# Page numbers of a decoder kernel: 64 loads into registers per layer, against sixteen packed words loaded once

## What is computed

```python
# _mix, for the sample group; past['k'] is (80 pages, 2 layers, 128, 8, 64)
pk = past['k'][past['page_table'], l].reshape(B, -1, SB_HEADS, SB_HEAD_DIM)
pv = past['v'][past['page_table'], l].reshape(B, -1, SB_HEADS, SB_HEAD_DIM)
P = pk.shape[1]
o_b = _sb_attend(q, concatenate([pk, k]), concatenate([pv, v]),
                 P + arange(T), arange(P + T), sbb)
# page_table: 64 of a permutation of 80, as int32
```

## Time and profile before

| | |
|---|---|
| median of 3 runs | 2043.45 us (2041.63 to 2048.05) |
| the profiled execution: its time | 2043.22 us |
| its span in the profile | 2041.4 us |
| busy share of the span | PE 91%, PEld 77%, DVE 47%, ACT 35%, POOL 4% |
| DMA | 391.48 MB, mean 192 GB/s |
| mean granted TensorE clock | 0.947 of full |

### The profile page before, as it was taken

One profiled execution on the slowest core, in us unless ns is written; L12 is line 12 of the kernel. 1 busy time (PEld: TensorE's weight loads), 2 busy tenths in 40 slices (PEclk: granted clock), 3 DMA queues, 4 the chain that ended last, 5 costly groups with the idle time before them and its releaser, 6 DMA issues. The chain is left out here.

```text
span 2041.4 us, 33570 instructions
## 1 busy us (share of the span) xinstructions
PE 1851.3 (91%) x12436; PEld 1567.1 (77%) x12436; DVE 965.1 (47%) x1749; ACT 720.3 (35%) x1317; POOL 81.7 (4%) x111
## 2 busy tenths in 40 slices
PE   6999989999987897999969999899999878979997
PEld 4988966776765686998959888667767656869997
DVE  4555425335355534555355553253353644346554
ACT  3554323323321103554345443233233211046552
POOL 0000010000000001000010000100000000010001
PEclk7999989999998998999979999999999888989999
DMA  7777642462348922456547776342641588325561
GB/s 320 279 281 293 252 170 84 167 232 109 134 154 211 272 104 101 166 200 254 226 165 271 299 292 227 146 161 81 237 183 59 165 256 224 110 99 174 213 229 69
DMA packets 87842, 391.48 MB, mean 192 GB/s; under 512 B 14402, under 2 KB 19778, under 8 KB 57410
## 3 DMA queue, kind: packets, MB, share of 16 engines
q1 hardware_dynamic: 72738, 368.24, 50.8%
q10 hardware_dynamic: 15008, 21.95, 2.9%
HBM read 377.32 MB, written 12.83 MB: 191 GB/s over the span
## 5 line engine op out<-in xcount | busy, mean ns | idle before, releaser
L982 DVE TENSOR_TENSOR ring_parts<-ring,pages_parts 128x1024 fp32r<-128x1024 f32 (+1 forms) x272 | 314.3, 1191 | 199.2 <-ACT pages_parts L1539 199.1
L451 PE MATMUL ps<-xn,ring 128*128 128x264 f32 x1664 | 400.0, 401 | 6.1 <-ACT xn L1546 6.1
L490 PE MATMUL ps<-arena_parts,pages_parts 128*128 128x264 f32 x1408 | 361.4, 292 | 23.5 <-DVE xn_parts L1050 21.1
L451 PEld LDWEIGHTS ps<-xn,ring 128*128 128x128 f32 x1664 | 326.9, 199 | 70.0 <-issue 10.4
L491 PE MATMUL ps<-xn_parts,pages_parts 128*128 128x264 f32 x1408 | 357.0, 288 | 0.0
L1539 ACT ACTIVATE pages_parts<-ring 128x1024 fp32r<-128x1024 f32 (+1 forms) x272 | 267.8, 1025 | 179.8 <-DMA ring<-in_w_ffn_in 71.8
L490 PEld LDWEIGHTS ps<-arena_parts,pages_parts 128*128 128x128 f32 x1408 | 271.8, 193 | 44.2 <-issue 43.6
L491 PEld LDWEIGHTS ps<-xn_parts,pages_parts 128*128 128x128 f32 x1408 | 271.2, 193 | 0.0
L495 PE MATMUL ps<-arena_parts,ring_parts 128*128 128x264 f32 x1408 | 196.5, 283 | 0.0
L490 PE MATMUL ps<-big_parts,pages_parts 128*128 128x264 f32 x704 | 177.6, 288 | 6.6 <-DVE gates_parts L996 6.6
L495 PEld LDWEIGHTS ps<-arena_parts,ring_parts 128*128 128x128 f32 x1408 | 181.9, 188 | 0.0
(11 more groups left out here) (312 smaller groups left out, 2039.6 us busy)
## 6 DMA issues: line engine op xcount, KB each, us to landing
ring<-in_w_ffn_in SPq DMA_DIRECT2D x88, 1024.0 KB, 4.9
ring<-in_w_ada SPq DMA_DIRECT2D x32, 1536.0 KB, 6.5
ring<-in_w_a SPq DMA_DIRECT2D x32, 1536.0 KB, 11.1
ring<-in_w_ffn_down SPq DMA_DIRECT2D x32, 1408.0 KB, 6.5
pages<-in_k_pages SPq DMA_DIRECT2D x128, 256.0 KB, 5.0
pages<-in_v_pages SPq DMA_DIRECT2D x128, 256.0 KB, 6.2
ring<-in_w_ada SPq DMA_DIRECT2D x24, 1024.0 KB, 7.2
ring<-in_w_proj SPq DMA_DIRECT2D x8, 1536.0 KB, 9.4
```

The source lines that it names most:

```text
L451: last = mm(ps[:, b, 0:T], tile_of(r, first + k), rhs(k), start=(k == 0), stop=(k == depth - 1))
L490: mm(ps[:, b, 0:T], tile, hi[:, k, :], start=start, stop=False)
L982: v.tensor_tensor(ring_lo[:, r, at * P:(at + n) * P], w, whi[:, place, 0:n * P].bitcast(F32), ALU.subtract)\
```

## The change

The DMA of the table now takes only the low byte of each number, 64 elements of one byte, so that four numbers lie in one 32-bit word of `ptab`. `read_tables` loads the sixteen words into sixteen registers once, in the first layer, after the loop over the first 16 FFN tiles. `page_number` takes a number out of its word with a shift and a mask, two register operations just ahead of the page's DMA. It is called between the wait and the issue. The hardware loop over the four heads is written out, since a register can't be chosen by a loop's index.

```diff
-        ptab = sb("ptab", [1, NB * PAGES], I32)
+        ptab = sb("ptab", [1, NB * PAGES // 4], I32)
+        ptab_bytes = ptab[:].bitcast(mybir.dt.uint8)
...
-                    sp.dma_start(ptab[:], ins.page_table).then_inc(S.t_in, 16)
+                    sp.dma_start(ptab_bytes.unsqueeze(2), ins.page_table.bitcast(mybir.dt.uint8)
+                                 .rearrange("p (n b) -> p n b", b=4)[:, :, 0:1],
+                                 allow_slow_non_contiguous=True).then_inc(S.t_in, 16)
...
+                def read_tables():
+
+                    sp.wait_ge(S.t_in, 48)
+                    packed.extend(sp.value_load(ptab[0:1, w:w + 1], min_val=0, max_val=(1 << 31) - 1)
+                                  for w in range(NB * PAGES // 4))
+
+                def page_number(n):
+
+                    number = sp.alloc_register()
+                    sp.reg_alu(number, packed[n // 4], 8 * (n % 4), ALU.logical_shift_right)
+                    sp.reg_alu(number, number, 127, ALU.bitwise_and)
+                    return sp.snap(number, donate=True, min_val=0, max_val=PHYS - 1)
...
+                if first_layer:
+                    read_tables()
                 for k in range(16, FC):
                     load(ins.w_ffn_in[layer, 0, k], 2)
...
-                if first_layer:
-                    sp.wait_ge(S.t_in, 48)
-                with sp.Fori(0, HEADS) as i, slots.loop(i, HEADS, [3] * 4), page_loads.loop(i, HEADS, 2):
-                    for k in range(3):
-                        load(ins.w_a[layer, i * 4 + k], 3)
-                    sp.wait_ge(S.yss_ready, 1)
-                    load_pages(ins.k_pages, i * 2)
-                    load(ins.w_a[layer, i * 4 + 3], 3)
-                    load_pages(ins.k_pages, i * 2 + 1)
...
+                for i in range(HEADS):
+                    for k in range(3):
+                        load(ins.w_a[layer, i * 4 + k], 3)
+                    sp.wait_ge(S.yss_ready, 1)
+                    load_key_pages(i * 2)
+                    load(ins.w_a[layer, i * 4 + 3], 3)
+                    load_key_pages(i * 2 + 1)
```

More of the change, by code:

```diff
@@ L291, in clear_all @@
             nc.all_engine_barrier()
+        packed = []
         def one_layer(block, layer):
@@ L307, in _ @@
             def _(sp):
-                slots, page_loads = Slots(), Count()
+                slots = Slots()
                 def start_loads():
@@ L331, in load @@
                     sp.dma_start(ring[:, r, 0:tiles * P], src).then_inc(slot_full[r], 16)
-                def load_pages(pool_of_pages, b):
-                    before = page_loads()
-                    numbers = [sp.value_load(ptab[0:1, bds(b * PAGES + j, 1)], min_val=0, max_val=PHYS - 1)
-                               for j in range(PAGES)]
-                    for j, page in enumerate(numbers):
-                        if j % 2 == 0:
-                            sp.wait_ge(page_free[j // 2], before + 1)
-                        sp.dma_start(pages[:, j, :], pool_of_pages[layer, page]).then_inc(page_full[j // 2], 16)
+                def read_tables():
[7 more added lines that the diff above has]
+                    return sp.snap(number, donate=True, min_val=0, max_val=PHYS - 1)
                 if first_layer:
@@ L361, in _, with load_key_pages, load_value_pages @@
                     load(ins.w_sq[layer, s], 2)
-                if first_layer:
-                    sp.wait_ge(S.t_in, 48)
-                with sp.Fori(0, HEADS) as i, slots.loop(i, HEADS, [3] * 4), page_loads.loop(i, HEADS, 2):
+                def load_key_pages(b):
+                    for j in range(PAGES):
+                        if j % 2 == 0:
+                            sp.wait_ge(page_free[j // 2], b + 1)
+                        sp.dma_start(pages[:, j, :], ins.k_pages[layer, page_number(b * PAGES + j)])\
+                            .then_inc(page_full[j // 2], 16)
+                def load_value_pages(b):
+                    for u in range(2):
+                        if b == 0:
+                            for j in range(4):
+                                sp.wait_ge(page_free[j], 2 * HEADS + 1)
+                        else:
+                            sp.wait_ge(value_free[u], b)
+                        for j in range(4):
+                            sp.dma_start(pages[:, 2 * j + u, :], ins.v_pages[layer, page_number(b * PAGES + 2 * j + u)])\
+                                .then_inc(value_full[u], 16)
+                for i in range(HEADS):
                     for k in range(3):
@@ L367, in _ @@
                     sp.wait_ge(S.yss_ready, 1)
-                    load_pages(ins.k_pages, i * 2)
+                    load_key_pages(i * 2)
                     load(ins.w_a[layer, i * 4 + 3], 3)
-                    load_pages(ins.k_pages, i * 2 + 1)
-                def load_value_pages(b):
-                    numbers = [sp.value_load(ptab[0:1, b * PAGES + j:b * PAGES + j + 1], min_val=0, max_val=PHYS - 1)
-                               for j in range(PAGES)]
-                    for u in range(2):
-                        if b == 0:
-                            for j in range(4):
-                                sp.wait_ge(page_free[j], page_loads.n + 1)
-                        else:
-                            sp.wait_ge(value_free[u], b)
-                        for j in range(4):
-                            sp.dma_start(pages[:, 2 * j + u, :], ins.v_pages[layer, numbers[2 * j + u]])\
-                                .then_inc(value_full[u], 16)
+                    load_key_pages(i * 2 + 1)
                 load(ins.w_b[layer, 0], 2)
```

## The result

| | before | after |
|---|---|---|
| median of 8 runs each | 2044.45 us (2041.63 to 2049.65) | 2058.6 us (2049.9 to 2064.55) |
| ratio, with its 95% interval | | 1.0068 [1.0049, 1.0086] |
| the profiled execution: its time | 2043.22 us | 2058.02 us |
| its span | 2041.4 us | 2056.2 us |
| mean granted TensorE clock | 0.947 | 0.949 |

A forecast was written before the change was run, and what follows sets the result against it. TensorE, busy 91% of 2041.4 us, was taken as the bound. 2043.2 - 0 (loads) + 1.4 (page operations) + 2.0 (FFN stall) + 0 (table DMA) = 2046.6, so 2046.8 against the median, 0.16% slower; range 2039 to 2052.5.

The forecast's parts named there:

- Sixteen loads take 9.0 us: First FFN: sixteen loads at 0.56 us each come ahead of tile 16's issue, ending at 140.9 with the branch.
- A tile needs 7.17 us from issue to its first piece: First FFN: time from a tile's issue to the end of VectorE's first piece, taken from tile 17; tile 16 ready at 148.1.
- TensorE began tile 16 at 146.09, so it needs it then: First FFN: tile 16, ready at 148.1, would stall TensorE once, +2.0 us, with ends of 0 and 4.0.
- The clock: nothing added, 0.9 or more at the upper end: TensorE's granted clock after the FFN stall: no loss added for a 2.0 us gap, 0.9 us or more at the upper end.
- For key pages this is hidden (no DMA wait at all): First mixer half: two register operations per page, 0.16 us, cost nothing; value pages pay 0.16 for each of nine waits, +1.4 us.
- upper end of 5.8: Second mixer half: the most the register operations on value pages could cost, 9 x 0.64 = 5.8 us.
- Gain from the 256 loads: 0: Mixer: removing the 256 register loads gains 0, with a bound of 3.5 us per layer, 7.
- Rival 3: Second mixer half: value sample 2's lateness was passed on, 3.5 us in each layer, so 2039.8; 9%.
- rival 2: Second mixer half: register loads slow the DMAs; some 23 us of waits would go, time near 2023; 5%.
- Rival 1, the byte elements: Start: the table's 64 one-byte elements block the DMA queue at 17 us, loads behind come 4.6 us later, 2051.4; 18%.

The follow-up runs named there:

- before_loads16: The kernel before with sixteen unused page-number loads added behind the loop over the first 16 FFN tiles of layer 1; 2048.54 us, ratio 1.0032.
- rows_first: The changed kernel with VectorE's copy to rbuf put ahead of its split of tile 16, the sixteen loads left in place; 2059.82 us, ratio 1.0053 to the kernel before.
- before_unrolled: The kernel before with its mixer loop over four heads written out, all 256 register loads kept; 2048.45 us, ratio 0.9995.
- mask_keys: The kernel before, loop written out, all loads kept, two register operations that change nothing ahead of each key page's DMA only; ratio 1.0010.
- late_ahead: The changed kernel with its sixteen loads moved into the mixer's first head and page numbers taken apart ahead of the waits; 2050.54 us, ratio 1.0015 to the kernel before.
- unrolled_mask: The kernel before, loop written out, all loads kept, two register operations that change nothing ahead of every page's DMA; 2048.2 us, ratio 1.0024.
- mask_values: The kernel before, loop written out, all loads kept, two register operations that change nothing ahead of each value page's DMA only; ratio 1.0002.
- fixed_pages: before_unrolled with constants for page numbers, so no register loads or operations for them and other pages read; 2042.76 us, ratio 0.9991 to the kernel before.
- late_table: late_ahead with the table's byte DMA issued behind the first FFN's loads, start waits for masks and sel alone; ratio 1.0024 to the kernel before.
- read_late: The changed kernel with its sixteen loads moved into the mixer's first head, behind the second load of w_a; 2046.27 us, ratio 1.0021 to the kernel before.

## Why the prediction was wrong, step by step

**"Sixteen loads take 9.0 us": right in kind, 0.5 short.** The timeline has 132.19 + 0.33 = 132.52 to 142.27, less the branch: 9.5 us or 0.59 each. The instructions are as long as in the earlier trace rows (a TENSOR_LOAD of 267 ns in the median, from 262 to 470). The lateness of 0.7 us that SyncE brings from the start comes on top, so tile 16 went out at 142.3 instead of 140.9. The figure of the Trainium skill, page "DMA: Bandwidth & Descriptors", section "Latency and other measured facts", some 600 ns for one `tensor_load`, would by the forecast's estimate have given 14 us. The measurement stands against it as a figure for the instruction, as the rows before did; a whole number, with its register operation, its check and the gaps, took 0.59 us.

**"A tile needs 7.17 us from issue to its first piece": right.** 142.27 to VectorE's first piece, which starts at 148.24 and takes half of 2.36, is 7.15 us.

**"TensorE began tile 16 at 146.09, so it needs it then": the step that failed.** The sum asked when TensorE wants the tile. It didn't ask what else stands behind the tile's split on VectorE. The copy to `rbuf` does (line 959 before), behind both pieces and not the first alone, and TensorE wants it before the tile. With the forecast's own numbers the right chain gives 140.9 + 7.17 + 1.18 (second piece) = 149.25, and 149.8 with the copy (0.55), against 145.84: a stall of 4.0, not 2.0. before_loads16 measured 4.21, and rows_first, with the order changed, 2.44.

**"The clock: nothing added, 0.9 or more at the upper end": mis-sized.** The stall was treated as nearer the short gap of the earlier trace rows, 1.20 us, and came out near the long one, 5.23. 1.7 us (1.3 in before_loads16) were lost behind it. A stall of the forecast's size might not have spared the clock either: in rows_first the gap was 2.44 us, and the granted clock was 0.50 from 149 to 152. Stall and clock are 6.3 us in the changed kernel's trace, and 6.5 by before_loads16's ratio.

**"For key pages this is hidden (no DMA wait at all)": the second step that failed.** That no wait is seen says that the room is not negative; it doesn't say how large it is. It was 0.16 to 0.91 us, less than what was added. The 0.16 us per page were right: the eight issues take 3.94 us in before_unrolled and 5.00 to 5.42 in mask_keys, 0.15 to 0.21 more per step. But the forecast counted only the first page's 0.16 for each wait, where TensorE waits for the last of eight, which comes 1.2 later. mask_keys shows the waits (3.3 us) and late_ahead takes them away (0). That they are most of the time lost is argued from these sums, since the ratio of mask_keys alone holds 1. Both kinds of pages together cost 4.9 us (unrolled_mask, 0.0024), where the forecast had 1.4 and put it all in the value pages, which alone cost nothing that can be told (mask_values). Its upper end of 5.8 held the size by luck, by another way.

**"Gain from the 256 loads: 0": right.** In fixed_pages, with no number read at all, the ratio is 0.9991 [0.9972, 1.0010], a gain of 1.8 us at best guess and 5.7 at most. Rival 3 (sample 2's lateness passed on, 7 us) falls with it, and so does rival 2 (the loads slow DMAs), which would have brought 20.

**Rival 1, the byte elements: refuted.** 400 GB/s around the table's DMA, `hmask` 0.8 us late, and no gain in late_table. The Trainium skill, the same page, section "Rules for kernel authors", lets one expect a descriptor for each of the 64 elements, and the traces agree: the changed kernel's has 64 DMA packets of one byte, from 18.65 to 19.19 us, where the kernel before has one of 256 bytes at 18.61. All 64 took under 1 us. The likeness to `out_n_p` didn't carry over from HBM to SBUF.

**The sum.** 6.5 us (before_loads16) and 4.9 (unrolled_mask) make 11.4 of 14 us, ratio 1.0056 against 1.0068 [1.0049, 1.0086]. The interval holds the sum, so nothing more is needed. But each part has an interval of its own of 4 us or so either way, and nothing forbids 2 or 3 us more that no run has named.

## What to carry to other kernels

When an instruction becomes late, take the list of its engine and ask who waits for each thing behind it, not only who waits for the thing itself: a small copy behind a late split stopped TensorE earlier and twice as long as the split would have. An operation with no wait on it has room of an unknown size; measure it as landing of the last part against use before calling an addition hidden, and add up all the pages of one stretch, not the first. Two register operations between a wait and its DMA are a price per transfer (0.15 us here): ahead of the wait they caused no waits here, though the time gained by that was too small to tell. And don't replace loads that nobody waits for.

## What was not expected of the hardware

**The mean granted clock and the mixer.** TensorE's same instructions ran the first mixer half at different granted clocks. The kernel before and read_late, the window 340 to 420:

```profile
340.00:420.00 80.00, 74.57 (x435) 56.90 (x434) 32.67 (x65) 27.06 (x48) 3.12 (x6) 0.96 0.40 152
```

```profile
340.00:420.00 80.00, 73.84 (x446) 57.13 (x445) 35.53 (x66) 27.11 (x48) 3.12 (x6) 1.00 0.43 158
```

read_late passed through this half 6.8 us quicker than the kernel before in spite of 3.3 us of waits for key pages. Its twelve runs went from 2032.24 us, at a mean clock of 0.956, to 2059.56, at 0.946, and in each of the other kernels, too, the slower runs have the lower clocks on the whole. So much of the scatter that hides costs of 0.2% goes with the clock, and one trace can't weigh them. read_late's median clock was 0.9515, and that of the kernel before on the same chip 0.948. This may be chance or an effect of the edit, no run tells which, and it makes read_late's 1.0021 a poor measure of what its loads and operations cost.
